# Two stacked layers on one core: the passage between them by token tile and in halves, and the output in four stores

## The reference, cut to what matters

```python
def second_block(x, ...):
    for l in range(DEPTH_2):                       # DEPTH_2 = 2
        h = rms_norm_2(x, norm_mix_pre[l])
        proj = h @ w_in[l]
        ...
        mix = jnp.concatenate([y_conf, y_sb, y_ret, y_sc], axis=-1) @ w_out[l]
        x = x + rms_norm_2(mix, norm_mix_post[l])
        f = conv_ffn(rms_norm_2(x, norm_ffn_pre[l]), ffn_up[l], ffn_conv_w[l], ffn_down[l])
        x = x + rms_norm_2(f, norm_ffn_post[l])
    return x

def rms_norm_2(x, g):
    xf = x.astype(jnp.float32)
    y = xf * lax.rsqrt(jnp.mean(xf * xf, axis=-1, keepdims=True) + NORM_EPS)
    return (y * g.astype(jnp.float32)).astype(x.dtype)
```

## Time and profile before

| | |
|---|---|
| median of three runs | 1401.66 us (1401.3 to 1404.6) |
| profiled execution, span from the first to the last instruction | 1403.2 us |
| mean granted clock of TensorE in it | 0.931 |
| TensorE (PE) busy with matmuls | 1193.6 us, 85% |
| weight loads (PEld) | 950.4 us, 68% |
| VectorE (DVE) | 735.2 us, 52% |
| ScalarE (ACT) | 483.1 us, 34% |

### The profile page before, as it was taken

The page is one execution under the profiler, slowest core; times in us unless marked ns, Lnnn a source line. Parts: engine busy times, 40 slices in busy tenths (PEclk is TensorE's granted clock), DMA queues, the critical chain, the costliest instruction groups (busy, mean ns, idle before and its releaser), DMA issues.

```text
span 1403.2 us, 22440 instructions
## 1 busy us (share of the span) xinstructions
PE 1193.6 (85%) x9455; PEld 950.4 (68%) x9455; DVE 735.2 (52%) x1144; ACT 483.1 (34%) x670; POOL 2.9 (0%) x12
## 2 busy tenths in 40 slices
PE   7989999899564745647456999999999999999998
PEld 6989798796221312213122799899999998899997
DVE  5474854375010101101011698887777898877776
ACT  4532432232000000000000554754445555744444
POOL 0000000000000000000000000000000000000000
PEclk9999999999887868878688999999999999999999
DMA  8831301698999999999999934586665435576650
GB/s 268 283 121 35 91 4 32 214 365 359 425 429 426 426 426 426 426 426 427 426 425 413 336 122 127 154 246 180 181 192 178 156 121 151 173 208 192 191 154 30
DMA packets 181560, 349.49 MB, mean 249 GB/s; under 512 B 8204, under 2 KB 154801, under 8 KB 168530
## 3 DMA queue, kind: packets, MB, share of 16 engines
q1 hardware_dynamic: 180970, 347.40, 68.4%
q10 hardware_dynamic: 488, 0.62, 0.2%
HBM read 346.93 MB, written 3.43 MB: 250 GB/s over the span
## 4 chain that ended last, share of the span: by engine, by line
PE 58%; DMA 17%; DVE 2%; SPq 2%; issue 1%; ACT 1%; DVEq 1%; ACTq 0%
PE ps L2636 24%; PE ps L2672 11%; DMA expert_ring<-in_w_expert_up 9%; PE ps L1836 6%; DMA expert_early<-in_w_expert_up 5%; PE ps L1867 3%; PE ps L1521 2%; DMA expert_ring<-in_w_expert_gate 2%; PE ps L1824 2%; PE ps L1881 2%; PE ps L2648 2%; PE ps L2610 2%; DMA expert_ring<-in_w_expert_down 1%; SPq L1971 1%; PE ps L211 1%
## 5 line engine op out<-in xcount | busy, mean ns | idle before, releaser
L1836 PE MATMUL ps<-expert_ring,w_slot 128*32 128x512 f32 x688 | 144.5, 724 | 118.6 <-DMA expert_ring<-in_w_expert_gate 39.8
L2984 DVE TENSOR_TENSOR w_lo<-expert_early,w_hi 128x2048 fp32r<-128x2048 f32 x80 | 182.8, 2291 | 26.1 <-ACT w_hi L2778 23.3
L1909 DVE TENSOR_TENSOR hT<-ps,hT 128x512 f32<-128x512 f32 x8 | 8.5, 1065 | 350.3 <-PE ps L1836 350.3
L2778 ACT ACTIVATE w_hi<-expert_early 128x2048 fp32r<-128x2048 f32 x80 | 153.0, 1919 | 56.8 <-PE ps L2672 34.1
L1836 PEld LDWEIGHTS ps<-expert_ring,w_slot 128*32 128x32 f32 x688 | 36.0, 130 | 190.6 <-issue 190.6
L2636 PE MATMUL ps<-x_hi,w_hi 128*128 128x256 f32 x960 | 134.2, 282 | 0.0
L2636 PE MATMUL ps<-x_hi,w_lo 128*128 128x256 f32 x960 | 134.1, 282 | 0.0
L2636 PE MATMUL ps<-x_lo,w_hi 128*128 128x256 f32 x960 | 132.3, 280 | 0.0
L1836 PE MATMUL ps<-expert_early,w_slot 128*32 128x512 f32 x256 | 91.5, 728 | 43.5 <-DMA expert_ring<-in_w_expert_gate 23.5
L2636 PEld LDWEIGHTS ps<-x_hi,w_hi 128*128 128x128 f32 x960 | 122.9, 188 | 3.8 <-issue 1.6
L2636 PEld LDWEIGHTS ps<-x_hi,w_lo 128*128 128x128 f32 x960 | 123.0, 190 | 0.0
(11 more groups left out here) (502 smaller groups left out, 2065.3 us busy)
## 6 DMA issues: line engine op xcount, KB each, us to landing
expert_ring<-in_w_expert_gate SPq DMA_DIRECT2D x22, 2048.0 KB, 23.9
expert_ring<-in_w_expert_up SPq DMA_DIRECT2D x21, 2048.0 KB, 26.6
expert_early<-in_ffn_up SPq DMA_DIRECT2D x36, 1024.0 KB, 6.2
expert_ring<-in_w_expert_down SPq DMA_DIRECT2D x16, 2048.0 KB, 26.7
w_slot<-in_w_in SPq DMA_DIRECT2D x28, 1024.0 KB, 5.5
expert_early<-in_w_in SPq DMA_DIRECT2D x20, 1024.0 KB, 5.2
expert_early<-in_ffn_down SPq DMA_DIRECT2D x18, 1024.0 KB, 5.0
expert_early<-in_w_expert_gate SPq DMA_DIRECT2D x8, 2048.0 KB, 24.4
```

What stands on the lines that cost most here:

```text
L1836: mm = pe.matmul(m.ps[rows_of(e), b, :], x_quad[:, k, rows_of(e)], w[e][:, k, :], start=(k == 0), stop=(k == KC - 1))
L2778: act.activation(w_hi[:, half_slot(l, i), :], raw_slot(m, i), ACT.Copy).then_inc(S["w_hi"], 1)
L2984: dve.tensor_tensor(w_lo[:, s, :], raw_slot(m, i), w_hi[:, s, :].bitcast(F32), ALU.subtract).then_inc(S["w_lo"], 1)
```

## The change

- Between the layers (l = 0): ScalarE takes, tile by tile, `root_of_sum("down", (t,))` and then `root_of_halves(4, t, ...)`, the root of the updated tile from two squares of 512 columns each. VectorE likewise: `post_norm("down", 6 + t, ...)` with two updates of 512 columns, then `scales(7 + t, (t,))`. The `root_of_state(0)` and `scales(0)` at the head of layer 1 go away. Three semaphores (`end_half`, `end_squared`, `end_eps`) are new.
- After the last layer (l = 1): the order on ScalarE is as before, VectorE updates x in halves and signals each half, and SyncE stores each half on its own, four stores of 256 KB.
- `post_norm` has no branch for the full width any more.

```diff
--- before.py
+++ after.py
@@ -2451,7 +2451,7 @@
              "conf_centred": 1, "conf_squared": 1, "conf_out": 1, "turned": 2, "sb_biased": 4, "soft_ln": 4, "sb_masked": 4,
              "sb_arg": 4, "sb_exp": 4, "ret_masked": 4, "ret_centred": 1, "ret_squared": 1, "conf_rooted": 1,
              "ret_rooted": 1, "tap_scaled": FF, "conv_done": FF, "silu_done": FF, "hid_done": FF,
-             "conf_normed": 1, "x_half": 2, "half_squared": 2, "half_eps": 2}
+             "conf_normed": 1, "x_half": 2, "half_squared": 2, "half_eps": 2, "end_half": 2, "end_squared": 2, "end_eps": 2}
     S = {n: sem(n) for n in total}
     pads_zero, gain_in, stored = (sem(n) for n in ("pads2_zero", "gain_in", "stored2"))
 
@@ -2549,9 +2549,11 @@
                     await_split(sp, 0, "w_lo", last)
                     load_piece(sp, m, a, 1, i)
         for t in range(TT):
-            sp.wait_ge(S["x_ready"], 2 * total["x_ready"] + t + 1)
-            sp.dma_start(out[0, t * P:(t + 1) * P, :], m.x_tok[:, t, :]).then_inc(stored, 16)
-        sp.wait_ge(stored, 16 * TT)
+            for c, (name, n) in enumerate((("end_half", total["end_half"]), ("x_ready", 2 * total["x_ready"]))):
+                sp.wait_ge(S[name], n + t + 1)
+                cols = slice(c * 512, (c + 1) * 512)
+                sp.dma_start(out[0, t * P:(t + 1) * P, cols], m.x_tok[:, t, cols]).then_inc(stored, 16)
+        sp.wait_ge(stored, 32 * TT)
 
     def layers_tensor(pe):
         for l in range(2):
@@ -2790,17 +2792,17 @@
                     act.activation(root[:, 0, t:t + 1], ss[:, 0, t, 0:1], ACT.Sqrt, bias=m.c("eps"), scale=1.0)
                     act.drain().then_inc(S["root"], 1)
 
-            def root_of_halves(first, t):
-
-                signalled(act, l, "x_half", t + 1)
+            def root_of_halves(first, t, names=("x_half", "half_squared", "half_eps")):
+
+                signalled(act, l, names[0], t + 1)
                 act.activation(junk[:, 0:512], m.x_tok[:, t, 0:512], ACT.Square, scale=D ** -0.5,
                                accum_out=ss[:, 0, t, 0:1])
-                act.drain().then_inc(S["half_squared"], 1)
+                act.drain().then_inc(S[names[1]], 1)
                 signalled(act, l, "x_ready", first + t + 1)
                 act.activation(junk[:, 512:D], m.x_tok[:, t, 512:D], ACT.Square, scale=D ** -0.5,
                                accum_out=ss[:, 0, t, 1:2])
                 act.drain()
-                signalled(act, l, "half_eps", t + 1)
+                signalled(act, l, names[2], t + 1)
                 act.activation(root[:, 0, t:t + 1], ss[:, 0, t, 1:2], ACT.Sqrt, bias=ss[:, 0, t, 0:1], scale=1.0)
                 act.drain().then_inc(S["root"], 1)
 
@@ -2819,8 +2821,7 @@
 
             if l == 0:
                 load_roots()
-            root_of_state(0)
-            if l == 0:
+                root_of_state(0)
                 split_piece(0)
             signalled(act, l, "vec_set", 1)
             for c in range(KC):
@@ -2925,7 +2926,10 @@
                 if kind == "up":
                     signalled(act, l, "conv_done", n + 1)
                     act.activation(silu[:, n % 2, :], ff[:, n % 2, 0, :], ACT.Silu).then_inc(S["silu_done"], 1)
-            root_of_sum("down")
+            for t in range(TT):
+                root_of_sum("down", (t,))
+                if l == 0:
+                    root_of_halves(4, t, ("end_half", "end_squared", "end_eps"))
 
     def layers_vector(dve):
 
@@ -2939,7 +2943,7 @@
                     dve.tensor_scalar(scale_eye[:, t, :], m.c("ident"), root[:, 0, t:t + 1], None, ALU.mult
                                       ).then_inc(S["scaled"], 1)
 
-            def post_norm(name, first, gains, tiles=range(TT), halves=False):
+            def post_norm(name, first, gains, tiles=range(TT), halves=None):
 
                 dve.wait_ge(gain_in, l * 32 + 16 * gains)
                 for t in tiles:
@@ -2952,19 +2956,16 @@
                     signalled(dve, l, "root", first + t + 1)
                     dve.reciprocal(root[:, 1, t:t + 1], root[:, 1, t:t + 1])
                     dve.drain()
-                    if not halves:
-                        dve.scalar_tensor_tensor(m.x_tok[:, t, :], added, root[:, 1, t:t + 1], m.x_tok[:, t, :],
-                                                 ALU.mult, ALU.add)
-                        dve.drain().then_inc(S["x_ready"], 1)
-                        continue
                     for c in range(2):
                         cols = slice(c * 512, (c + 1) * 512)
                         dve.scalar_tensor_tensor(m.x_tok[:, t, cols], added[:, cols], root[:, 1, t:t + 1],
                                                  m.x_tok[:, t, cols], ALU.mult, ALU.add)
-                        dve.drain().then_inc(S["x_ready" if c else "x_half"], 1)
-                    signalled(dve, l, "half_squared", t + 1)
+                        dve.drain().then_inc(S["x_ready" if c else halves[0]], 1)
+                    if len(halves) == 1:
+                        continue
+                    signalled(dve, l, halves[1], t + 1)
                     dve.tensor_scalar(ss[:, 0, t, 0:1], ss[:, 0, t, 0:1], m.c("eps"), None, ALU.add)
-                    dve.drain().then_inc(S["half_eps"], 1)
+                    dve.drain().then_inc(S[halves[2]], 1)
 
             def split_y(c):
 
@@ -2995,7 +2996,8 @@
                             dve.scalar_tensor_tensor(conf[:, c, :], src, tap, conf[:, c, :], ALU.mult, ALU.add)
                     dve.drain()
 
-            scales(0)
+            if l == 0:
+                scales(0)
             dve.tensor_copy(vec[:, :], vec_next[:, :])
             dve.tensor_copy(ff_taps[:, :, :], taps_next[:, :, :])
             dve.drain().then_inc(S["vec_set"], 1)
@@ -3125,7 +3127,7 @@
             split_low(15)
             split_low(PIECE_FFN)
             for t in range(TT):
-                post_norm("out", 2 + t, 1, (t,), halves=True)
+                post_norm("out", 2 + t, 1, (t,), ("x_half", "half_squared", "half_eps"))
                 scales(4 - 1 + t, (t,))
             for c in range(KC):
                 if c % 2 == 0:
@@ -3170,7 +3172,12 @@
                     split_low(PIECES)
                 if kind == "up":
                     hidden(n)
-            post_norm("down", 6, 2)
+            if l == 0:
+                for t in range(TT):
+                    post_norm("down", 6 + t, 2, (t,), ("end_half", "end_squared", "end_eps"))
+                    scales(7 + t, (t,))
+            else:
+                post_norm("down", 6, 2, range(TT), ("end_half",))
 
     m.x_ready = S["x_ready"]
     return layers_gpsimd, layers_sync, layers_tensor, layers_scalar, layers_vector
```

## The result

The changed kernel takes 1408.91 us in the median of five runs (1406.46 to 1409.12), the kernel before 1401.82 in the median of five (1401.3 to 1404.6). The ratio of the runs to those of before is 1.0032, with a 95% interval of 1.0019 to 1.0045: 4.5 us slower, between 2.7 and 6.3.

What follows compares the result with a forecast made beforehand. TensorE was taken as the bound, with no wait left in layer 1 to absorb delay. 2.28 + 0.27 + 0.03 = 2.58 us, 4.2 with a short clock fall, put on the 1401.66 median: 1405.9 us, range 1403.6 to 1408.0.

Steps and rivals of the forecast that it cites:

- The delay through ScalarE's queue: Passage into layer 1: tile 1's sums queue behind tile 0's norm, so the first product comes 2.28 us later.
- x_lo behind the low split: Start of layer 1: VectorE reaches x_lo later, so its first matmul waits 0.27 us more, zero at best.
- The hole and the clock: TensorE idles 3.28 us between the two tiles' turns; its granted clock then likely halves, costing up to 1.65 us.
- short fall: Behind TensorE's hole the clock is halved for 3.3 us, costing up to 1.65 us; total 1405.9 us, chance 0.39.
- The end: Last layer: half updates delay the last half 0.68 us, its smaller store saves 0.65; net +0.03 us.
- SP's queue: Gain load and next weights in layer 1 wait for later work but keep step with TensorE; costed at nothing.
- The sum: Whole kernel: 2.58 us slower without a clock fall, 4.2 with a short one, 5.6 with a long one.
- the overlap wins: Rival: tile 1's sums don't wait for tile 0's norm, first product 0.35 us early; 1400.7 us, chance 0.05.
- The delay is absorbed: Rival: a later wait in layer 1 swallows 2.6 us, so no change, 1401.7 us; chance 0.04.
- The clock holds: Rival: TensorE's clock doesn't fall around the hole between the turns; 1404.2 us, chance 0.25.
- the long fall: Rival: 6.6 us at half the clock around TensorE's hole, costing about 3.0 us; 1407.2 us, chance 0.27.

Runs made afterwards that it cites:

- e3: Changed kernel with three more matmuls of ones on TensorE between tile 0's and tile 1's turn; ratio 1.0017 to the kernel before.
- e4: Changed kernel's passage between layers with updates and squares in halves, but both tiles' sums first, then both norms, as before; ratio 1.0014 to the kernel before.

## Why the prediction was right, point by point

- **The delay through ScalarE's queue** (2.28): right. Tile 0's second sum to tile 1's first is 4.43 us for 4.45; tile 1's second sum to its turn 4.99 for 5.01; with the clock held the first product stands 13.21 us behind tile 0's first sum, for 0.98 + 12.25.
- **x_lo behind the low split** (0.27): right as part of the sum in e3, whose P is 19.34 for 16.79 + 2.55. It shows in e3 as 0.26. In the changed kernel TensorE doesn't wait for x_lo at all: at half the clock it comes late itself, which is part of why the fall cost less than half of its stretch.
- **The hole and the clock** (1.65, short fall likeliest): the hole is 3.38 us for 3.28, the fall came in four of four profiles, always the short one. Its cost is 1.23 us. The term was mis-sized by 0.4: half of the low stretch was taken, without the wait of 0.26 us for x_lo that it covers. That leaves 1.4, and the last 0.2 I can't place.
- **The end** (0.03): 0.06. Two delays of 0.34 us on VectorE against 0.6 from half the bytes. The sentence from the Trainium skill would have made it 0.68; a half store took 2.0 us here, not 2.6.
- **SP's queue** at nothing: right, 290.62 us between P and E for 290.60.
- **The sum**: 4.2 us predicted. The trace gives 3.78 + 0.06 = 3.84, and the ratios 4.5 (2.7 to 6.3) and 3.8 us (2.2 to 5.5). The mechanism and the sum are right. The ratios alone hardly tell the short fall (4.2) from the long one (5.6) or from the clock that holds (2.6); the traces do. What the range missed is the base: I put the difference on a median of three runs, 1401.66, 2 to 3 us low, and gave the executions' own scatter too little room. One of the two ratios, 1.0032, is just above the 0.3% that the prediction named as its line, the other, 1.0027, just below.
- **The rivals**: *the overlap wins* fell at the point named for it, as tile 1's first sum came 3.1 us later. *The delay is absorbed* is out by the stretch between P and E. *The clock holds* and *the long fall* were seen in no execution of this kernel; the first is what e3 makes by hand.

## What to carry to other kernels

Going tile by tile pays only if the next tile's input comes late enough: work that is put between two tiles on an engine's queue holds the second tile back until it is done, waits included. Compare its length, from tile 0's first sum to the point where tile 1's can start, with the distance at which the producer delivers the tiles. Here that is 5.4 us against 2.8 (at the end of layer 1, where ScalarE waits for each bank, the first sums of the two tiles start at 1392.99 and 1395.76 in the kernel before), and tile 1 comes 3.1 us late. In the passage that the order was copied from it is 5.9 (1196.99 to 1202.84) against 5.6, and the order gains 0.3 us. And when a turn is split in two, look at the hole that opens between the parts: at 3.4 us it cost a fall of TensorE's clock on top. For an edit of a few microseconds in a kernel whose executions scatter by as much, read the local length between two fixed instructions.

## What the runs showed of the hardware that I had not expected

Holes of 2.06 and 2.63 us were followed by a fall of the clock, one of 2.83 was not the earlier trace rows, nor was the one of 2.46 in e4; after 3.38 to 3.46 us it was lost four times of four, for about 3.4 us each, from 0.3 us ahead of the next matmul to 0.8 behind it. A store of 256 KB landed in 2.0 us when it was issued 0.9 us behind another and in up to 2.3 when 0.4 behind, one of 512 KB in 2.6. The start of the passage, behind the expert layers, scattered by 5 us between executions of the same instructions.
